# The gated delta recurrence takes solved matrix times (values less gated keys times state), and its last solving level makes the transposed matrix directly

## The reference

```
decay  = exp(gc_i - gc_j) on and below the diagonal;  gc = cumsum(g)
a_mat  = strict lower part of beta * (k k^T) * decay
t_mat  = inverse of (I + a_mat)
w_c    = t_mat @ (beta * k * exp(gc))
u_c    = t_mat @ (beta * v)
qk     = (q k^T) * decay
# step over the chunks:
v_new  = u_c - w_c @ state
o      = (q * exp(gc)) @ state + qk @ v_new
state  = state * exp(g_last) + (k * exp(g_last - gc))^T @ v_new
```

## Time and profile before

| what | value |
|---|---|
| median of 3 runs | 2462.41 us (2459.09 to 2471.61) |
| the profiled execution | 2464.8 us |
| its span, first to last instruction | 2462.7 us |
| mean granted TensorE clock | 0.978 |
| busy share of the span: TensorE, VectorE, ScalarE, GpSimd | 97%, 44%, 32%, 31% |

### The profile page before, as it was taken

How to read it: one execution, slowest core, us unless ns; L and a number is a source line. 1 busy time by engine, 2 the same in 40 slices (tenths; PEclk the granted TensorE clock), 3 DMA queues, 4 the chain that set the end, 5 groups by cost and what they waited for, 6 DMA issues and landing times.

```text
span 2462.7 us, 32786 instructions
## 1 busy us (share of the span) xinstructions
PE 2376.7 (97%) x12918; PEld 2023.8 (82%) x12918; DVE 1076.2 (44%) x1656; ACT 792.3 (32%) x1346; POOL 766.4 (31%) x544
## 2 busy tenths in 40 slices
PE   7999998899799999999999999999999999999999
PEld 5788886899787888887888878978888788888887
DVE  5166654555436534452222252133333343556633
ACT  4145453222412422232222221144443112665101
POOL 2212232554222677743222223221111241111250
PEclk8999999999898999999999989999999999999999
DMA  7722222222531335353332106533431346434341
GB/s 240 214 60 69 61 68 57 77 59 59 183 134 43 110 113 173 118 185 112 97 103 64 56 18 236 134 86 105 115 107 54 121 171 152 111 98 154 128 154 69
DMA packets 265531, 274.95 MB, mean 112 GB/s; under 512 B 44114, under 2 KB 221048, under 8 KB 263593
## 3 DMA queue, kind: packets, MB, share of 16 engines
q1 hardware_dynamic: 243368, 217.32, 29.5%
q10 hardware_dynamic: 22016, 55.61, 6.2%
HBM read 188.91 MB, written 86.08 MB: 112 GB/s over the span
## 4 chain that ended last, share of the span: by engine, by line
PE 92%; DVE 2%; DMA 2%; ACT 1%; issue 1%; POOL 0%; SPq 0%; POOLq 0%; DVEq 0%; ACTq 0%
PE PS L301 18%; PE PS L2082 13%; PE PS L282 11%; PE PS L2063 10%; PE PS L2390 4%; PE PS L3193 4%; PE PS L3049 4%; PE PS L2345 3%; PE PS L409 2%; PE PS L2603 2%; PE PS L2095 2%; PE PS L1458 2%; PE PS L1464 2%; PE PS L719 1%; PE PS L2592 1%; PE PS L2888 1%
## 5 line engine op out<-in xcount | busy, mean ns | idle before, releaser
L249 POOL CAST Wh<-Wraw 128x1024 fp32r<-128x1024 f32 x72 | 75.7, 1052 | 904.0 <-PE PS L301 599.1
L2082 PE MATMUL PS<-op_h,fw_h 128*128 128x512 f32 x512 | 199.5, 390 | 2.1 <-POOL fw_l L1977 2.1
L2082 PE MATMUL PS<-op_h,fw_l 128*128 128x512 f32 x512 | 199.5, 390 | 0.0
L2082 PE MATMUL PS<-op_l,fw_h 128*128 128x512 f32 x512 | 199.4, 390 | 0.0
L251 POOL TENSOR_TENSOR Wl<-Wraw,Wh 128x1024 fp32r<-128x1024 f32 x72 | 176.2, 2448 | 10.4
L1977 POOL TENSOR_TENSOR fw_l<-draw,fw_h 128x512 fp32r<-128x512 f32 x64 | 84.7, 1326 | 253.8 <-ACT fw_h L2118 253.8
L1977 POOL TENSOR_TENSOR fw_l<-fraw,fw_h 128x512 fp32r<-128x512 f32 x92 | 125.9, 1382 | 94.6 <-ACT fw_h L2118 94.5
L2063 PE MATMUL PS<-op_h,fw_h 128*128 128x512 f32 x392 | 152.7, 390 | 0.0
L2063 PE MATMUL PS<-op_l,fw_h 128*128 128x512 f32 x392 | 152.7, 390 | 0.0
L2063 PE MATMUL PS<-op_h,fw_l 128*128 128x512 f32 x392 | 152.7, 390 | 0.0
L2307 DVE TENSOR_TENSOR hT<-hT,PS 128x1024 f32<-128x1024 f32 x32 | 39.1, 1221 | 220.4 <-PE PS L2082 220.4
(11 more groups left out here) (494 smaller groups left out, 5968.6 us busy)
## 6 DMA issues: line engine op xcount, KB each, us to landing
Wraw<-in_w_in SPq DMA_DIRECT2D x66, 512.0 KB, 4.4
fraw<-in_w_ffn_in SPq DMA_DIRECT2D x16, 1024.0 KB, 5.3
f_scr<-blocks SPq DMA_DIRECT2D x16, 1024.0 KB, 4.3
draw<-in_w_ffn_out SPq DMA_DIRECT2D x32, 512.0 KB, 4.1
stage<-f_scr SPq DMA_DIRECT2D x24, 512.0 KB, 4.5
x_scr<-hT SPq DMA_DIRECT2D x2, 4096.0 KB, 13.1
Wraw<-in_w_out SPq DMA_DIRECT2D x16, 512.0 KB, 3.7
gate_scr<-gbuf ACTq DMA_DIRECT2D x16, 512.0 KB, 2.7
```

What stands on the lines that cost most here:

```text
L249: pool.tensor_copy(Wh[:, slot], Wraw[:, slot])
L2082: mm = pe.matmul(dense_bank(n)[:, 512 * b:512 * b + 512], w_, x_, start=(k == 0 and m == 0), stop=(k == KT - 1 and m == 2))
```

## The change

- GpSimd no longer makes the gated keys (`k_gated` is gone), TensorE no longer forms `w` from them (line 1481), and ScalarE no longer copies `wTn`.
- In the last level (n = 6) the X product takes all 128 columns of `W`, and the mask on VectorE covers 128 columns for each head. The second product has X and `U` with the roles turned round, 128 columns wide, and gives the correction of the transposed matrix: VectorE subtracts it from `U` in place. The last level has no transposes and no copies of them on ScalarE.
- A step first forms keys times state (`keys_state`); VectorE turns it into gated keys times state less values, in one fused instruction for each head (`values_less_state`, buffer `Vs`, four for each direction), `U` times that gives the negated new values, and ScalarE copies them with scale -1. `keys_state` of the pair's first step stands between the X products and the second products of the last level. Queries times state stands behind the values' product in the first step of a pair, and ahead of it in the second.
- In pairs 1 and 2 `solve(p + 1)` runs its first two parts in level 5, two more at the end of level 6, and the last two in the second step, behind the gating of the queries' product; before, all were done by the end of `levels`. In pair 0 all are done by the end of `levels` in both.
- SyncE waits for the last values' product instead of the last `w` before it loads `w_out`.

```diff
             def k_gated(p):            # removed, with its three calls
-                    pool.tensor_tensor(kg[e][d], heads(ktok[:, t]), gates_of(eg[:, d], d, t), ALU.mult)
...
@@ pe levels(p)
+                    last = n == LEVELS - 1
...
                         for h in range(GH):
-                            mm = pe.matmul(bank(d, e)[:, h * 64:(h + 1) * 64], KdTs[p % 2][e][d][:, h],
-                                           joined(W_of(p, e, d)[:, h], n, d), start=True, stop=True)
+                            if last:
+                                mm = pe.matmul(bank(d, e)[:, h * P:(h + 1) * P], KdTs[p % 2][e][d][:, h], W_of(p, e, d)[:, h],
+                                               start=True, stop=True)
...
+                    if last:
+                        if p == 0:
+                            pe.wait_ge(zeros_made, 2)
+                        keys_state(2 * p)
...
+                            if last:
+                                mm = pe.matmul(bank(d, e)[:, h * P:(h + 1) * P], Xs[e][d][:, h], U_of(p, e, d)[:, h],
+                                               start=True, stop=True)
...
-                    for e, d in four:
-                        pe.wait_ge(d_w[d], i + e + 1)
+                    for e, d in four if not last else ():
+                        pe.wait_ge(d_w[d], i - 2 * p + e + 1)
...
-                for e, d in four:
-                    pe.wait_ge(d_u[d], 2 * NL * p + 2 * NL - 1 + e)
-                    pe.wait_ge(d_kg[d], 2 * p + e + 1)
+            def keys_state(s):
+                for d in range(2):
+                    t = chunk(d, s)
+                    if s:
+                        pe.wait_ge(d_st[d], s)
                     for h in range(GH):
-                        mm = pe.matmul(bank(d, 2 + e)[:, h * P:(h + 1) * P], kg[e][d][:, h], U_of(p, e, d)[:, h],
+                        mm = pe.matmul(bank(d, 2)[:, h * P:(h + 1) * P], Craw[:, 4 + h, t * P:(t + 1) * P], St[d][:, h],
                                        start=True, stop=True)
-                    mm.then_inc(d_wt[d], 1)
+                    mm.then_inc(d_ks[d], 1)
 
             def steps(p):
+                def from_state(s):
                     for d in range(2):
                         t = chunk(d, s)
...
+                        if s % 2:
                             pe.wait_ge(d_o1r[d], s)
+                        else:
+                            pe.wait_ge(d_u[d], 2 * NL * (p + 1))
                         for h in range(GH):
                             mm = pe.matmul(bank(d, 1)[:, h * P:(h + 1) * P], Craw[:, h, t * P:(t + 1) * P], St[d][:, h],
                                            start=True, stop=True)
                         mm.then_inc(d_o1[d], 1)
+
+                for e in range(2):
+                    s = 2 * p + e
+                    if e:
+                        keys_state(s)
+                        from_state(s)
+                    for d in range(2):
+                        pe.wait_ge(d_u[d], 2 * NL * p + 2 * NL - 1 + e)
+                        pe.wait_ge(d_vs[d], s + 1)
+                        for h in range(GH):
+                            mm = pe.matmul(bank(d, 0)[:, h * P:(h + 1) * P], U_of(p, e, d)[:, h], Vs[d][:, h],
+                                           start=True, stop=True)
+                        mm.then_inc(d_v[d], 1)
+                    if e == 0:
+                        from_state(s)
...
@@ act
-                for e, d in four:
-                    act.wait_ge(d_wt[d], 2 * p + e + 1)
-                    act.activation(wTn[e][d], heads(bank(d, 2 + e)), ACT.Copy, scale=-1.0).then_inc(d_wtn[d], 1)
...
-                    act.activation(W_of(p, e, d), heads(bank(d, 0)), ACT.Copy).then_inc(d_vn[d], 1)
+                    act.activation(W_of(p, e, d), heads(bank(d, 0)), ACT.Copy, scale=-1.0).then_inc(d_vn[d], 1)
...
@@ dve
+            def values_less_state(s):
+                for d in range(2):
+                    t = chunk(d, s)
+                    dve.wait_ge(d_ks[d], s + 1)
+                    if s:
+                        dve.wait_ge(d_v[d], s)
+                    for h in range(GH):
+                        g = 8 * t + 4 * d + h
+                        ins = dve.scalar_tensor_tensor(Vs[d][:, h], bank(d, 2)[:, h * P:(h + 1) * P], eg[:, d, g:g + 1],
+                                                       Craw[:, 8 + h, t * P:(t + 1) * P], ALU.mult, ALU.subtract)
+                    ins.then_inc(d_vs[d], 1)
...
+                    if last:
+                        values_less_state(2 * p)
+                    elif p == 0 or n > LV0:
                         next(solving, None)
                     for e, d in four:
                         dve.wait_ge(d_wx[d], i + e + 1)
+                        if last:
+                            u = U_of(p, e, d)
+                            dve.tensor_tensor(u, u, heads(bank(d, e)), ALU.subtract).then_inc(d_u[d], 1)
+                            continue
...
                     if p == 0 or n > LV0:
                         next(solving, None)
-                for _ in solving:
-                    pass
-
-            def steps(p):
+                    if last:
+                        next(solving, None)
+
+            def steps(p, solving):
                 for e in range(2):
                     s = 2 * p + e
                     t1 = KdTs[p % 2][e]
+                    if e:
+                        values_less_state(s)
                     for d in range(2):
                         dve.wait_ge(d_o1[d], s + 1)
                         dve.tensor_tensor(t1[d], heads(bank(d, 1)), gates_of(eg[:, d], d, chunk(d, s)), ALU.mult
                                           ).then_inc(d_o1r[d], 1)
+                    for _ in solving if e else ():
+                        pass
                     for d in range(2 if s + 1 < NT else 0):
```

More of the change, by code:

```diff
@@ L1196, in build @@
         WY_all, WT_all = [WY0_all, WY1_all], [WT0_all, WT1_all]
-        kg, _ = units("kg", 96)
+        Vs = [sb(f"Vs{d}", [P, GH, P], F32, 96 + 2 * d) for d in range(2)]
         dec, _ = units("dec", 104)
@@ L1373, in pool_phase4 @@
             qk_masked(0)
-            for d in range(2):
-                pool.wait_ge(d_dt[d], 4)
-            k_gated(0)
             pool.wait_ge(mm_done, N_OUT1)
@@ L1457, in levels @@
                         for h in range(GH):
-                            mm = pe.matmul(bank(d, e)[:, h * 64:(h + 1) * 64], KdTs[p % 2][e][d][:, h],
-                                           joined(W_of(p, e, d)[:, h], n, d), start=True, stop=True)
+                            if last:
+                                mm = pe.matmul(bank(d, e)[:, h * P:(h + 1) * P], KdTs[p % 2][e][d][:, h], W_of(p, e, d)[:, h],
+                                               start=True, stop=True)
+                            else:
+                                mm = pe.matmul(bank(d, e)[:, h * 64:(h + 1) * 64], KdTs[p % 2][e][d][:, h],
+                                               joined(W_of(p, e, d)[:, h], n, d), start=True, stop=True)
                         mm.then_inc(d_x[d], 1)
+                    if last:
+                        if p == 0:
+                            pe.wait_ge(zeros_made, 2)
+                        keys_state(2 * p)
                     for e, d in four:
@@ L1463, in levels @@
                         for h in range(GH):
-                            mm = pe.matmul(bank(d, e)[:, h * 64:(h + 1) * 64], U_of(p, e, d)[:, h],
-                                           Xs[e][d][:, h, 0:64], start=True, stop=True)
+                            if last:
+                                mm = pe.matmul(bank(d, e)[:, h * P:(h + 1) * P], Xs[e][d][:, h], U_of(p, e, d)[:, h],
+                                               start=True, stop=True)
+                            else:
+                                mm = pe.matmul(bank(d, e)[:, h * 64:(h + 1) * 64], U_of(p, e, d)[:, h],
+                                               Xs[e][d][:, h, 0:64], start=True, stop=True)
                         mm.then_inc(d_wx[d], 1)
-                    for e, d in four:
-                        pe.wait_ge(d_w[d], i + e + 1)
+                    for e, d in four if not last else ():
+                        pe.wait_ge(d_w[d], i - 2 * p + e + 1)
                         if n == LV0:
@@ L1556, in act_phase4 @@
                 for n in range(NL):
-                    for e, d in four:
-                        act.wait_ge(d_ut[d], 2 * (NL * p + n) + e + 1)
+                    for e, d in four if n < NL - 1 else ():
+                        act.wait_ge(d_ut[d], 2 * ((NL - 1) * p + n) + e + 1)
                         act.activation(U_of(p, e, d), heads(bank(d, 2 + e)), ACT.Copy).then_inc(d_u[d], 1)
@@ L1625, in levels @@
                     shape = dict(h=GH, b=64 >> n, c=1 << n)
+                    last = n == LEVELS - 1
                     for e, d in four:
                         dve.wait_ge(d_x[d], i + e + 1)
```

(9 more changed lines are left out.)

37 lines of the change are left out of this document (8 added, 29 removed).

## The result

| kernel | median us (lowest to highest, runs) | ratio to before, 95% interval |
|---|---|---|
| before | 2461.54 (2459.09 to 2471.61, 4) | 1 |
| changed | 2475.39 (2473.49 to 2477.37, 4) | 1.0044, 1.0027 to 1.0061 |

The account below looks back on a forecast made before the run. TensorE's gapless work was taken as the bound: -21.3 + 0.4 (copies) + 2.7 (late state) + 10.65 and 2.6 (stops) + 2.5 (low clock) = -2.5 us, median 2460 us, range 2446 to 2472 for 8 in 10.

Parts of the forecast that it names:

- low clock's term: Behind TensorE's stop ahead of the fourth pair, half of 5.1 us at the 1.2 GHz level is lost: +2.5 us.
- 10.65 us stop: Ahead of the fourth pair (index 3), TensorE waits for solved blocks coming late through memory: +10.65 us.
- shorter stop ahead of pair 3: Ahead of the third pair (index 2), TensorE waits 1.1 then 1.5 us for solved blocks: +2.6 us.
- TensorE's own sum: Transposes and four groups removed, widening free: 5.33 us less in each of four pairs, -21.3 us.
- Fused instructions: VectorE's new 128 x 128 instructions making `Vs` take 0.25 us each in a series, 1.0 us for a direction.
- VectorE rival: VectorE bounds the recurrence through slower fused instructions: 12 us in all at 0.5 us each, 2472; chance 0.15.
- Solve late: Last two solver parts, behind the second step's gating, end 25.9 us after the third pair's last level starts.
- State late: GpSimd slows solver parts on VectorE, so the next keys product waits 0.9 us in three pairs: +2.7 us.
- `Wraw`: At the phase's end, the later issue of this load costs 0; as a rival +4.6 us, 2464, chance 0.10.
- +0.4 for ScalarE's copies: In each pair's second step, the copy of new values is not fully covered: 0.1 us a pair.
- Hidden trip: Rival: solved blocks still arrive through memory in time, leaving -18 us, 2444; chance 0.13.

Follow-up runs that it names:

- widened level: Changed kernel with level 4 of the third and fourth pair done over all 128 columns of each head: 2459.71 us, ratio to before 0.9978.
- delayed kernel before: Kernel before, with six more waited-for stores of the solved blocks ahead of storing them for the third and fourth pair: 2496.55 us, ratio 1.0142.
- trip taken away: Changed kernel storing the solver's starting blocks for the last two pairs, the solver's work kept on unread tiles: 2441.99 us, ratio to before 0.9912.
- new last level alone: Kernel before with only the transposed, 128-column last level without transposes; recurrence and solver places unchanged: 2458.91 us, ratio 0.9994.
- first experiment: Changed kernel with TensorE running 3 and 13 groups of unread products in its stops ahead of the third and fourth pair: 2468.53 us, ratio 1.0017.

## Why the prediction was wrong

The step that failed is the low clock's term. The text said that after the 10.65 us stop "half of 5.1, 2.5 us, is lost", and gave the shorter stop ahead of pair 3 no such cost. Measured: 9.0 and 8.2. With these the same sum gives -2.5 + 14.7 = +12.2 on before, against +13.9 measured by the medians and +10.8 by the ratio. I took the length of the low stretch from the earlier trace rows, where transposes stood first behind the stop and one narrow group ran low behind them; here eight groups of 64 columns stand first, and they ran 13.7 us at the low level. The widened level shows what other work does behind the same stop (11.2 us in place of 17.1); the delayed kernel before shows that the loss doesn't need the change's code. What I used as a constant depended on the work behind the stop, and not on that alone: in one execution the clock stayed low for some 19 us behind the very stop that the 5.1 was read from.

The Trainium skill ("TensorE: Matmul & The Clock Gate", section "HAM oscillation — how this bites in real kernels") puts the loss at the low time multiplied by one minus 1.2/2.4. The trace agrees: 17.07 us low cost 8.23, 0.48 of it.

The other steps:

- *TensorE's own sum*: right. Wide and narrow groups stand 0.89 apart. With the trip taken away the trace gains 17.6 us where 18.2 were left, and the new last level alone gains 7.1, the transposes' 7.0.
- *Fused instructions*: right, and with them the VectorE rival falls, although the result is near its 2472. VectorE's timeline of the changed kernel in the third pair, and then GpSimd's of the same time, with the columns of the timelines above:

```profile
580.38 2.16 DVE L1634 SCALAR_TENSOR_TENSOR Vs<-PS,eg,Craw 128x128 f32<-128x128 f32 x8 [0.20 <-PE PS L1484]
...
587.37 0.23 DVE L1617 TENSOR_TENSOR blkU<-blkA,blkY 128x63 f32<-128x63 f32 x1
587.66 1.02 DVE L1620 TENSOR_TENSOR blkY<-blkY,blkU 128x63 f32<-128x63 f32 x1
588.76 0.93 DVE L1617 TENSOR_TENSOR blkU<-blkA,blkY 128x64 f32<-128x64 f32 x1
...
594.28 2.15 DVE L1634 SCALAR_TENSOR_TENSOR Vs<-PS,eg,Craw 128x128 f32<-128x128 f32 x8
...
601.51 0.38 DVE L1624 COPY blkT<-blkY 128x256 f32<-128x256 f32 x1
```

```profile
587.57 2.04 POOL L1383 TENSOR_TENSOR St<-St,eg 128x512 f32<-128x512 f32 x2 [35.59 <-PE PS L1497]
593.84 2.51 POOL L1390 TENSOR_TENSOR oacc<-oacc,KdT 128x512 f32<-128x512 f32 x2 [4.23 <-DVE KdT L1691]
```

 Eight fused instructions take 2.16 us, 0.27 each against 0.25 taken. The second series lies wholly beside GpSimd's additions (593.84 to 596.35) and takes 2.15: with a factor and one operand in SBUF it is not held. The solver's operations with both operands in SBUF are, 1.02 and 0.93, while GpSimd decays the state: two in that time, as forecast.
- *Solve late*: it ends at 601.89, 26.2 us behind the last level's start; forecast 25.9. The stops followed from it within 1 us; ahead of the third pair it was one stop of 2.45 and not 1.1 and 1.5, as the slow groups covered the wait for the e = 1 blocks.
- *State late*: idle times of 0.76, 0.48 and 0.48; counted from where the group before gives way 0.9, 0.6 and 0.6, at or a little under the 0.9 each.
- *`Wraw`*: right. The chain of the changed kernel, in order of time, answers to the earlier trace rows:

```profile
661.83 0.38 SPq L207
662.21 0.05 issue
662.26 9.11 DMA Wraw<-in_w_out
```

 The issue is 17.3 us later (662.26 against 644.93), 4.0 of them beyond the recurrence's own 13.3, but the landing, 671.37 against 658.62, is only 12.75 later: the transfer was 4.6 us shorter, and the later issue costs nothing.
- *The last step*: the +0.4 for ScalarE's copies took it that "what waits behind it is only the update". The last step has no update, and its output waits for the copy, 0.8 us.
- *Hidden trip*: no; its 2444 is close to what the kernel without the trip gives, 2442.0.

The Trainium skill ("GPSIMD Engine Reference", section "4.1 Engine selection") would have elementwise work on VectorE, GpSimd being about twice as slow with two inputs. The trace has 0.31 against 0.22 for the solver's operations, less than that, and the kernel that moves them is the fastest, since the idle engine's time was free.

## What to carry to other kernels

In these traces a stop of TensorE had two prices, the wait and the low clock behind it. The second must be read from work like that which follows the stop, and from more than one execution: narrow fp32 products stayed slow for 14 us where wide ones were back in 3 to 6. When a chain is moved behind other work, lay out its whole trip to the consumer, and look for an idle engine to run it on before accepting the stop. If a stop can't be avoided, put the widest products first behind it.

## What the runs showed of the hardware

- Idle times of 2.3 and 11.4 us ahead of 64-column products cost nearly the same behind them, 8.2 and 9.0 us at the 1.2 GHz level. Ahead of 128-column products, with idle times of 2.4 and 11.0, it was 1.6 and 2.4 (first level widened).
- The same stop of 6.3 us with the same work behind it was followed by some 5 us at the low level in the kernel before and by some 19 us in the delayed kernel before (441.22 to 460.66).
- Gaps of 0.79 and 1.08 us with two narrow groups between them were followed by the low level (first experiment), and so were 1.92 and 1.41 (the delayed kernel before); 1.29 alone was not (first experiment, third pair). So here the clock was lost by short waits for data among narrow products.
- A group of four heads' fp32 products takes 0.89 us at 64 and at 128 columns at full clock, and at the low level too the spacing is nearly the same (1.71 between the narrow ones, 1.70 between the second and third wide one, 604.31 to 606.01).
